# The out product of a pooling mixer, three of its four groups as seven block products

## The reference

```python
h = x @ w_in                                   # 1024 x 4096
u, z = h[..., :2048], h[..., 2048:]
# four groups of 512 columns, windows 2, 4, 8, 16: m = window mean of u, minus u
m = einsum('bsgc,gcd->bsgd', m, w_grp).reshape(B, S, 2048) * scale     # "group product"
y = (m * silu(z)) @ w_out                      # 1024 x 2048 @ 2048 x 1024, "out product"
out = layer_norm(2 ** 0.25 * x + y, g, b)
```

## Time and profile before

| | |
|---|---|
| median of 3 runs | 1905.43 us (1902.81 to 1905.44) |
| the profiled execution | 1901.53 us, its span 1899.7 us |
| TensorE busy | 1845.9 us, 97% of the span |
| VectorE busy | 1286.1 us, 68% |
| ScalarE busy | 614.3 us, 32% |
| GpSimd busy | 1020.2 us, 54% |
| mean granted clock | 0.994 |
| Pool output stage | from 1622.2, matmuls end at 1883.8 |

### The profile page before, as it was taken

How to read it: one execution, slowest core, us unless ns; L and a number is a source line. 1 busy time by engine, 2 the same in 40 slices (tenths; PEclk the granted TensorE clock), 3 DMA queues, 4 the chain that set the end, 5 groups by cost and what they waited for, 6 DMA issues and landing times. The chain is left out here.

```text
span 1899.7 us, 23560 instructions
## 1 busy us (share of the span) xinstructions
PE 1845.9 (97%) x8976; PEld 1552.5 (82%) x8976; DVE 1286.1 (68%) x1473; ACT 614.3 (32%) x1110; POOL 1020.2 (54%) x783
## 2 busy tenths in 40 slices
PE   7999999999999999999999999999999999999996
PEld 7889889987887888888878887787788888888885
DVE  6777135566687776576599989567888785654446
ACT  4422157762331111111133334315432433311114
POOL 3443322252049988898777875532754565334245
PEclk9999999999999999999999999999999999999998
DMA  6121110023231233233376431113232333823322
GB/s 173 46 56 45 42 21 20 19 63 115 89 100 67 80 120 118 71 126 120 109 280 230 145 122 45 45 45 133 89 121 91 123 110 125 315 70 134 133 67 89
DMA packets 120163, 195.27 MB, mean 103 GB/s; under 512 B 30064, under 2 KB 85872, under 8 KB 116992
## 3 DMA queue, kind: packets, MB, share of 16 engines
q1 hardware_dynamic: 119888, 193.34, 30.0%
q10 hardware_dynamic: 176, 0.59, 0.1%
HBM read 145.08 MB, written 48.82 MB: 102 GB/s over the span
## 5 line engine op out<-in xcount | busy, mean ns | idle before, releaser
L820 POOL TENSOR_TENSOR cols<-ones 128x1 f32<-128x1 f32 x60 | 25.6, 426 | 297.3 <-PE ps L1018 272.7
L823 POOL TENSOR_TENSOR w_lo<-stage,w_hi 128x1024 fp32r<-128x1024 f32 x60 | 155.3, 2589 | 5.0
L1018 PE MATMUL ps<-f_hi,ring_hi 128*128 128x512 f32 x384 | 149.7, 390 | 1.3 <-POOL ring_lo L913 1.3
L1018 PE MATMUL ps<-f_hi,ring_lo 128*128 128x512 f32 x384 | 149.4, 389 | 0.0
L1018 PE MATMUL ps<-f_lo,ring_hi 128*128 128x512 f32 x384 | 149.4, 389 | 0.0
L1018 PE MATMUL ps<-d_w_hi,d_hid_hi 128*128 128x512 f32 x312 | 121.9, 391 | 4.2 <-DVE y L2468 1.5
L913 POOL TENSOR_TENSOR ring_lo<-w_sum,ring_hi 128x512 fp32r<-128x512 f32 x80 | 119.4, 1492 | 6.7
L1018 PE MATMUL ps<-d_w_hi,d_hid_lo 128*128 128x512 f32 x312 | 121.5, 389 | 0.0
L1018 PE MATMUL ps<-d_w_lo,d_hid_hi 128*128 128x512 f32 x312 | 121.4, 389 | 0.0
L976 POOL TENSOR_TENSOR ring_lo<-w_sum,ring_hi 128x512 fp32r<-128x512 f32 x60 | 93.9, 1575 | 43.4 <-ACT ring_hi L1906 43.4
L1018 PE MATMUL ps<-u_hi,w_hi 128*128 128x512 f32 (+1 forms) x288 | 106.3, 369 | 3.7 <-DVE u_lo L2061 3.7
(11 more groups left out here) (416 smaller groups left out, 5481.1 us busy)
## 6 DMA issues: line engine op xcount, KB each, us to landing
d_raw<-hid_rows SPq DMA_DIRECT2D x37, 512.0 KB, 4.5
stage<-in_w_up SPq DMA_DIRECT2D x22, 512.0 KB, 4.5
wd_raw<-in_w_down SPq DMA_DIRECT2D x22, 512.0 KB, 4.8
raw_w<-in_w_gate SPq DMA_DIRECT2D x20, 512.0 KB, 5.0
stage<-in_w_in SPq DMA_DIRECT2D x18, 512.0 KB, 3.7
stage<-in_pool_w_in SPq DMA_DIRECT2D x16, 512.0 KB, 5.2
raw_w<-in_pool_w_in SPq DMA_DIRECT2D x16, 512.0 KB, 4.8
m_rows<-u_row SPq DMA_DIRECT2D x16, 512.0 KB, 2.6
```

The source lines that it names most:

```text
L820: g.tensor_tensor(token, ones[:, 0:1], ones[:, 0:1], ALU.mult)
L823: g.tensor_tensor(lo, stage[:, h, :], hi.bitcast(F32), ALU.subtract).then_inc(parted[h], 1)
L1018: last = mm(out_ap, l, r, start=(start and j == 0), stop=(stop and j == n - 1), skip_group_check=onto)
```

## The change

For groups 0 to 2 (`STD_G = 3`) the out product of 1024 rows x 512 by 512 x 1024 is cut into 2 x 2 blocks of 512 x 256 by 256 x 512 and done as seven block products of Strassen's algorithm in Winograd's form, Q1, Q2, Q6, Q5, Q7, Q3, Q4. Group 3 stays as it was, and the low parts of its rows are still made for each gated block. In the seven:

- Gated rows are written over `z_in` (there is no `gt`). Four sums of row blocks (`g_sums`) are made on VectorE, three over `z_in` blocks, one in `g_diff`; four sums of weight blocks (`out_sums`) over the raw blocks `wo_raw` and in `wo_sum`. None goes through DRAM.
- Each of the seven operands of rows and of weights (128x1024) gets its high part from ScalarE and its low part from GpSimd, but for the rows of Q6, Q7 and Q3, whose low parts VectorE makes. They rotate through four slots each (`o_g`, `d_w`).
- Q1, Q6, Q5, Q7 start a bank; Q2 accumulates onto Q1's banks, Q3 onto Q5's, Q4 onto Q7's, each after those have been added. Q1, Q1+Q2 and so on are added by VectorE, 28 additions a group: Q1 and Q6 into `y2_both` (summed over the groups, and copied the first time), the others into their quarter of `y2`. At the end `y2_both` is added to three quarters of `y2` (`out_both_add`, 12 times): 8 in the last changed group, 4 in group 3.
- The loads are by block (`wo_load`, 512 KB each, rows of 2 KB), and `z_load` by halves, each issued when what lay there has been read.
- The low parts of the next group's `m` come behind the additions of Q5, Q7, Q3 and Q4.

```diff
+        y2_both = at("y2_both", [P, 4, HALF], Z)
+        def out_bank(o):
+            return 4 if o in (Q6, Q7, Q4) else 0
+        def out_split_by_dve(o):
+            return o in (Q6, Q7, Q3)
+        def w_out_block(o):
+            return (wo_raw[0], wo_raw[2], wo_sum, wo_raw[0], wo_raw[1], wo_raw[3], wo_sum)[o]
+        def g_block(o):
+            if o == Q7:
+                return g_diff[:]
+            e, n = {Q1: (0, 0), Q2: (1, 0), Q6: (0, 0), Q5: (0, 1), Q3: (1, 0), Q4: (1, 1)}[o]
+            return z_in[:, e, 2 * n:2 * n + 2, :]
...
 SP
+            sp.wait_ge(prod_full, quad_full(LAST_Q, 5))
+            for b in (0, 1, 3, 2):
+                wo_load(0, b)
             sp.wait_ge(prod_full, quad_full(LAST_Q, 6))
-            out_load(0, 0)
...
+                z_load(g, 0)
...
+                lo_done(e, Q3)
+                lo_done(e, Q4)
+                z_load(g, 1)
+            for r in range(2):
+                load(T_POOL + GROUPS + r, rows_tile(pw_out, GW * PHASE[STD_G] + 256 * r))
...
 GpSimd
+            part(T_POOL, 1, landed(T_POOL))
+            for i in range(STD_G):
+                out_weight_lo(i, Q1)
+                out_weight_lo(i, Q2)
+                out_rows_lo(i, Q1)
+                out_weight_lo(i, Q6)
+                out_rows_lo(i, Q2)
+                out_weight_lo(i, Q5)
+                out_rows_lo(i, Q5)
+                out_weight_lo(i, Q7)
+                pool.wait_ge(grp_full, 8 * i + 8)
+                part(T_POOL + i + 1, 1, landed(T_POOL + i + 1))
+                out_weight_lo(i, Q3)
+                out_weight_lo(i, Q4)
+                out_rows_lo(i, Q4)
+            pool.wait_ge(out_full, OUT_ADDS - 4)
+            part(T_POOL + GROUPS, 2, landed(T_POOL + GROUPS))
+            pool.wait_ge(out_full, OUT_ADDS)
+            part(T_POOL + GROUPS + 1, 0, landed(T_POOL + GROUPS + 1))
...
 TensorE
+            def out_blocks(g, o, i):
+                if o in (Q1, Q6):
+                    pe.wait_ge(gt_ready, 8 * g + out_bank(o) + i + 1)
+                else:
+                    pe.wait_ge(y2_added, 28 * g + 4 * out_before(o) + i + 1)
+                (h_hi, h_lo), (w_h, w_l) = o_g[(7 * g + o) % 4], d_w[(7 * g + o) % 4]
+                onto = o in (Q2, Q3, Q4)
+                terms = [(h_hi[:, k, i * P:(i + 1) * P], h_lo[:, k, i * P:(i + 1) * P], w_h[:, k, :], w_l[:, k, :])
+                         for k in range(2)]
+                three(ps[:, out_bank(o) + i, :], terms, start=not onto, onto=onto).then_inc(out_full, 1)
...
+                if g < STD_G:
+                    for o in range(7):
+                        pe.wait_ge(w_split, OUT_W + 7 * g + o + 1)
+                        pe.wait_ge(d_lo_dve if out_split_by_dve(o) else d_lo_pool, out_split_at(g, o))
+                        for i in range(4):
+                            out_blocks(g, o, i)
...
 ScalarE
+            for g in range(STD_G):
+                out_weight_hi(g, Q1)
+                out_weight_hi(g, Q2)
...
+                out_rows_hi(g, Q1)
+                out_weight_hi(g, Q6)
+                out_rows_hi(g, Q2)
+                out_weight_hi(g, Q5)
+                out_rows_hi(g, Q6)
+                out_rows_hi(g, Q5)
+                out_weight_hi(g, Q7)
+                out_rows_hi(g, Q7)
+                pool_rows_hi(g + 1, (0, 1))
+                out_weight_hi(g, Q3)
+                out_rows_hi(g, Q3)
+                pool_rows_hi(g + 1, (2,))
+                out_weight_hi(g, Q4)
+                out_rows_hi(g, Q4)
+                pool_rows_hi(g + 1, (3,))
...
 VectorE
+            def out_sums(g, i):
+                b11, b12, b21, b22 = (wo_raw[b][:] for b in range(4))
+                if i == 0:
+                    dve.wait_ge(wd_in[0], wo_landed(g, 0))
+                    dve.wait_ge(wd_in[1], wo_landed(g, 1))
+                    dve.wait_ge(w_split, OUT_W + 7 * g + Q1 + 1)
+                    ins = v.tensor_tensor(b11, b12, b11, ALU.subtract)
...
+                else:
+                    dve.wait_ge(wd_in[2], wo_landed(g, 2))
+                    dve.wait_ge(w_split, OUT_W + 7 * g + Q6 + 1)
+                    ins = v.tensor_tensor(wo_sum[:], b21, wo_sum[:], ALU.subtract)
...
+            for g in range(STD_G):
                 dve.wait_ge(z_back, 32 * g + 32)
                 for j in range(8):
+                    gated(g, j)
+                    if 1 <= j <= 3:
+                        out_sums(g, j - 1)
+                    if j == 4:
+                        out_sums(g, 3)
+                    if j == 5:
+                        g_sums(g, 0)
+                g_sums(g, 1)
+                g_sums(g, 2)
+                for o in range(7):
...
+                    for i in range(4):
+                        out_add(g, o, i)
+                    if o == Q1:
+                        out_rows_low(g, Q6)
+                    if o == Q2:
+                        g_sums(g, 3)
+                    if o == Q6:
+                        out_rows_low(g, Q7)
+                    if o == Q5:
+                        out_rows_low(g, Q3)
+                    if o >= Q5:
+                        pool_rows_lo(g + 1, o - Q5)
+                    if g == STD_G - 1 and o >= Q7:
+                        for j in ((), (0, 1), (2, 3, 4), (5, 6, 7))[o - Q5]:
+                            out_both_add(j)
```

More of the change, by code:

```diff
@@ L1515, in pe_program @@
                         ts = slice(n * HALF, (n + 1) * HALF)
-                        terms = [(w_hi[s][:, k * 512 + m * P:k * 512 + (m + 1) * P],
-                                  w_lo[s][:, k * 512 + m * P:k * 512 + (m + 1) * P],
+                        terms = [(w_hi[1][:, k * 512 + m * P:k * 512 + (m + 1) * P],
+                                  w_lo[1][:, k * 512 + m * P:k * 512 + (m + 1) * P],
                                   m_hi[:, k, ts], m_lo[:, k, ts]) for k in range(4)]
                         three(ps[:, b, :], terms).then_inc(grp_full, 1)
[L1520 to L1541, removed]
@@ L1961, in first_block_rows, with pool_rows_hi @@
                 f(u_row[0][:, HALO:HALO + HALF], ps[:, 0, :], ACT.Copy).then_inc(c11_ready, 1)
-            def pool_rows_hi(g):
+            def pool_rows_hi(g, parts=range(4)):
                 if g:
                     act.wait_ge(grp_full, 8 * g)
-                for k in range(4):
+                for k in parts:
                     if k % 2 == 0:
@@ L2009, in act_program, with out_slot_free @@
                     next_hi(q + 1, 5 + j)
[L2011 to L2021, removed]
+            def out_slot_free(g, o):
+                s = 7 * g + o
+                if s < 4:
+                    act.wait_ge(prod_full, quad_full(LAST_Q, (1, 3, 5, 6)[s]))
+                else:
+                    act.wait_ge(out_full, 4 * (s - 4) + 4)
@@ L2023, in act_program @@
+            act.wait_ge(out_full, OUT_ADDS)
+            for j in range(8):
+                act.wait_ge(gt_ready, 8 * STD_G + j + 1)
+                f(g_hi[:, j % 4, half(j // 4)], z_in[:, j % 4 // 2, j % 2 + 2 * (j // 4), :], ACT.Copy).then_inc(g_hi_ready, 1)
             for t in range(TB):
@@ L2670, in scale_deviations, with gated @@
                                        ALU.mult, ALU.add).then_inc(out_ready, 1)
-            for g in range(GROUPS):
-                n8 = 8 * g
+            def gated(g, j):
+                m, n = j % 4, j // 4
+                rows = z_in[:, m // 2, m % 2 + 2 * n, :]
+                dve.wait_ge(grp_full, 8 * g + j + 1)
+                v.scalar_tensor_tensor(rows, ps[:, j, :], pool_gain[:, 4 * PHASE[g] + m:4 * PHASE[g] + m + 1],
+                                       rows, ALU.mult, ALU.mult).then_inc(gt_ready, 1)
@@ new lines, in out_rows_low, with out_add @@
+            def out_rows_low(g, o):
+                src, (hi, lo) = g_block(o), o_g[(7 * g + o) % 4]
+                dve.wait_ge(d_hi, N_DOWN + 7 * g + o + 1)
+                v.tensor_tensor(lo[:], src, hi[:].bitcast(F32), ALU.subtract).then_inc(d_lo_dve, 1)
+            summed = {}
+            def out_add(g, o, i):
+                t, n = {Q2: (i, 0), Q5: (4 + i, 1), Q7: (4 + i, 1), Q3: (i, 1), Q4: (4 + i, 0)}.get(o, (8, i))
+                rows = y2_both[:, i, :] if t == 8 else y2[:, t, half(n)]
+                at_add = 28 * g + 4 * o + i + 1
+                dve.wait_ge(out_full, at_add)
+                if t == 8 and (t, n) not in summed:
+                    v.tensor_copy(rows, ps[:, out_bank(o) + i, :]).then_inc(y2_added, 1)
+                else:
+                    if (t, n) in summed:
+                        dve.wait_ge(y2_added, summed[t, n])
+                    v.tensor_tensor(rows, ps[:, out_bank(o) + i, :], rows, ALU.add).then_inc(y2_added, 1)
+                summed[t, n] = at_add
@@ L2686, in dve_program @@
[L2686 to L2690, removed]
-                        dve.wait_ge(y2_in, 64)
[L2692 to L2712, removed]
@@ new lines, in dve_program, with gated_low @@
+            dve.wait_ge(z_back, 32 * STD_G + 32)
```

(29 more changed lines are left out.)

183 lines of the change are left out of this document (142 added, 41 removed).

## The result

The changed kernel takes 1912.2 us (median of 5 runs, 1910.9 to 1913.9), the kernel before 1903.0 (5 runs, 1901.7 to 1905.4). The ratio is 1.0045 with a 95% interval of 1.0031 to 1.0060: slower by 9.2 us. The profiled execution took 1913.9, its span 1912.1.

A forecast was written before the change was run, and what follows sets the result against it. TensorE's matmuls were taken to bound the stage, 0.227 us each. Terms: -16.3 removed, +7.8 group 0, +7.4 first two boundaries, +8.0 last boundary, +4.5 clock = +11.4 us, 1916.8 on a 1905.4 median; range 1903 to 1924.

The forecast's parts named there:

- What is removed: Out products of three groups: 72 fewer matmuls at 0.227 us each, saving 16.3 us.
- Group 0: TensorE stands before Q2, waiting for VectorE's first addition of Q1 behind held sums: 7.8 us, bounds 0 to 11.
- the forecast chain: Group 0: block arrivals, GpSimd low parts, held VectorE sums, then the first addition of Q1, ending at 1657.2.
- exclusion: VectorE and GpSimd exclude each other when both read SBUF; a held VectorE sum costs up to 2.4 us more.
- Inside groups 1 and 2: Q2 in these groups: no stall, 0.3 us to spare, upper bound 1 us each.
- Boundaries 1 and 2: Group products of groups 1 and 2 wait for m's fourth low part: 3.7 us each, 2.5 to 5.
- The last boundary: Into group 3, `y2_both` additions and GpSimd's tile delay the last low part: 8 us, bounds 4.5 to 11.
- The clock: Matmuls at half clock behind pauses: 1.5 us at group 0 and last boundary, half that at two others; 4.5, 0 to 8.
- only the boundaries count: Rival: group 0 and clock cost nothing, boundaries cost 2.5, 2.5 and 4.5; -6.8 us, 1898.6; chance 0.14.
- its deciding point: Group 0: the only-boundaries rival holds if the first addition of Q1 starts before 1651.
- One large stall absent: Rival: group 0's stall missing, or last boundary only 2.5 us; +2.1 or +4.4, 1907.5 to 1909.8; chance 0.16.

The follow-up runs named there:

- the two last versions: Changed kernel, group products started before the fourth low part and two group 0 weight sums later: 1893.3 us; also that low part made earlier: 1890.6 us.
- the memset run: Changed kernel with five of group 0's GpSimd low parts set to zero by an operation that reads nothing: 1902.1 us, one profiled execution.
- two edits, one on TensorE and one on VectorE: Changed kernel, 18 group-product matmuls ahead of the fourth low part's wait: 1897.0 us; changed kernel, that low part made before Q4's additions: 1901.9 us.
- The fill run: Changed kernel with small matmuls on constants in the gaps, 60 ahead of Q2 in group 0, 25 ahead of each later group product: 1906.3 us.

## Why the prediction was right, point by point

The forecast was slower by 11.4 us, 1916.8 on a median of 1905.4. Measured is +9.2, and +10.1 in the stage of the profiled runs.

- *What is removed:* 72 matmuls, 1152 to 1080 in the stage, 16.3 us. Right: the account of the stage closes with it, and the two last versions keep 10 to 12 us of it.
- *Group 0:* 7.8 forecast, 7.77 measured, by the forecast chain. The stage started 2.3 later than in the trace that I worked from; with that added, Q1's weights were due at 1637.3 and came at 1637.45, the first addition was due at 1659.5 and ended at 1659.4. That GpSimd's low parts make it is shown by the memset run, and that the order of the sums does by the run that moves two of them. How much of it is exclusion is estimated (5.4 of 7.8) and not measured by itself.
- *Inside groups 1 and 2:* no stall forecast, none measured.
- *Boundaries 1 and 2:* 3.7 each forecast, 4.17 and 2.90 measured, 7.1 against 7.4. The mechanism is shown by two edits, one on TensorE and one on VectorE. The lateness above 2.5 was argued from a low part of m that the next group's Q1 weights hold; the memset run shows that at the first boundary it came from group 0. There m 1 is held as before (3.39 us), and the boundary still costs only 2.53.
- *The last boundary:* 8.0 forecast, 4.55 measured, the term that was most mis-sized. The half tile landed when I took it to (GpSimd starts at 1822.0, 1.5 us before the end of Q4). But two of the three `y2_both` additions slipped in ahead of it, and the last low part was not held:

```profile
1820.42 1.22 DVE L2760 TENSOR_TENSOR m_lo<-m_in,m_hi 128x1024 fp32r<-128x1024 f32 x1
1821.55 2.73 DVE L2890 TENSOR_TENSOR y<-y,y_both 128x512 f32<-128x512 f32 x3
1824.21 2.47 DVE L2883 TENSOR_TENSOR y<-ps,y 128x512 f32<-128x512 f32 x4
1826.60 1.21 DVE L2760 TENSOR_TENSOR m_lo<-m_in,m_hi 128x1024 fp32r<-128x1024 f32 x1
```

  These rows are VectorE in order of time there. The three additions of 0.68 took 2.73 where I had 4.8, and the last low part started 0.1 us after GpSimd's had ended, where I had it held.
- *The clock:* 4.5 forecast, 7.0 measured. It fell behind three cuts, not behind the one of 2.9, and cost 1.6, 2.7 and 2.6 where I had 1.5, 0.75 and 1.5 (and 0.75 at the one of 2.9): behind the first boundary and the last one 13 matmuls ran at the lower clock, 5.6 us, while my row had 3.4 in all. The Trainium skill's advice in "TensorE: Matmul & The Clock Gate", "Why this matters for your kernels", to avoid idle gaps between bursts of matmuls is borne out by this trace at those three. The fill run, which keeps the cuts and loses most of the price, shows that the idleness has this price.
- *The rivals:* "only the boundaries count" is out, Q2 of group 0 did wait; its deciding point, a first addition before 1651, was missed by 5 us after taking off the shift. "One large stall absent" is out too, although the last one was nearer to its lower bound of 4.5 than to my 8. The two errors, -3.5 at the last boundary and +2.5 on the clock, nearly cancelled. That is luck, and it makes the sum better than its terms. There is luck in the clock's term by itself too, since the same pause did not cost the same in every run (last section). One slip: 7 x 5.45 + 21.8 is 59.9 us for a changed group, not 59.8, which moves nothing.

## What to carry to other kernels

A saving of matmuls on a bound TensorE is real money, but it is paid back at each place where TensorE waits for one operation that stands behind its own last result; look for the operand that is prepared last and put independent matmuls ahead of its wait. In a queue written by hand, an operation goes no earlier than its consumer needs it: sums for Q7 and Q4 in front of the addition for Q2 cost more than their own length, since each was held by GpSimd. Where a VectorE operation takes both inputs from SBUF while GpSimd reads SBUF too, plan the two as one engine: 1.2 us became up to 3.4 here, while additions out of PSUM kept their 0.6 to 0.7. And give a pause of TensorE its price in slow matmuls: those of 4.2 to 7.8 us cost 1.3 to 2.9 us more in these runs.

## What the runs showed that I had not expected

The stretch at the lower clock was longer than in the row that I had used: 13 matmuls of 0.43 us behind cuts of 4.2 and 4.6 us. Nor did the length of a pause of about 3 us decide. The cut of 2.90 at the second boundary left the clock at 1.00 in the changed kernel. The same cut, 2.91 us, lost it in the memset run and cost 1.6 us; granted clock behind it, columns as above:

```profile
1751.40:1755.40 4.00, 4.00 (x11) 3.12 (x12) 0.00 (x0) 0.00 (x0) 0.00 (x0) 0.58 0.82 289
```

A pause of 3.4 us that ends at about 1189.5, where the programs are the same, kept 1.00 in the profiled execution before and lost it in the one after (0.66 in the mean from 1186.1 to 1196.0). The price varies too: the last boundary's cut of 4.6 us cost 2.6 in the changed kernel and 1.3 in the memset run. So a term for the clock behind a pause of this kind was uncertain by 1 to 1.6 us here, with the program known.

Matmuls of 128 columns on constants, at some 0.11 us each, were enough to hold the clock over a pause of 7.6 us. A GpSimd memset of 128x1024 took 0.95 us and held no VectorE sum. GpSimd's copy into the high part did hold VectorE: the `y2_both` addition that met the copy of 1822.26 took 1.53 us in place of 0.68.
